# Gate and up products of an expert, interleaved block by block of the contraction

## The reference

```
xe = hf[idx]
hid = jax.nn.silu(jnp.einsum('ecd,edf->ecf', xe, w_gate)) * jnp.einsum('ecd,edf->ecf', xe, w_up)
ye = jnp.einsum('ecf,efd->ecd', hid, w_down) * gates[..., None].astype(h.dtype)
```

## Time and profile before

| | |
|---|---|
| time, median of 3 runs | 1726.99 us (1726.78 to 1728.21) |
| profiled execution, first to last instruction (span) | 1722.5 us |
| what lies around the span, by the runs' median | 4.5 us |
| PE busy, weight loads busy | 1557.6 us, 1324.2 us |
| DVE, ACT, POOL busy | 1111.9, 807.8, 158.4 us |
| mean share of the DMA engines while the experts run | 0.75 to 0.79 |

### The profile page before, as it was taken

One profiled execution on the slowest core, in us unless ns is written; L12 is line 12 of the kernel. 1 busy time (PEld: TensorE's weight loads), 2 busy tenths in 40 slices (PEclk: granted clock), 3 DMA queues, 4 the chain that ended last, 5 costly groups with the idle time before them and its releaser, 6 DMA issues.

```text
span 1722.5 us, 22530 instructions
## 1 busy us (share of the span) xinstructions
PE 1557.6 (90%) x8435; PEld 1324.2 (77%) x8435; DVE 1111.9 (65%) x1529; ACT 807.8 (47%) x1046; POOL 158.4 (9%) x168
## 2 busy tenths in 40 slices
PE   7699999789979878299999999999999999999990
PEld 1588888366748766088899899989988998899880
DVE  2554443647668957747777676777677776767754
ACT  3522332422342232256566665666565655666543
POOL 2011100000000000001011011101110111011100
PEclk9799999989989988689999999999999999999995
DMA  9144341435233135157878777877877787878728
GB/s 348 52 131 127 111 124 61 159 115 191 98 87 84 43 132 192 52 189 229 266 227 256 214 256 237 255 226 249 250 241 239 234 253 228 266 221 249 234 88 311
DMA packets 233220, 324.03 MB, mean 188 GB/s; under 512 B 9892, under 2 KB 193264, under 8 KB 233176
## 3 DMA queue, kind: packets, MB, share of 16 engines
q1 hardware_dynamic: 221784, 297.32, 51.9%
q0 software_dynamic: 9280, 25.47, 7.1%
q10 hardware_dynamic: 2112, 0.66, 0.2%
HBM read 291.90 MB, written 31.51 MB: 188 GB/s over the span
## 4 chain that ended last, share of the span: by engine, by line
PE 78%; DVE 12%; DMA 3%; SPq 2%; ACT 2%; issue 1%; POOL 0%; DVEq 0%; POOLq 0%; ACTq 0%
PE ps L1183 23%; PE ps L926 21%; PE ps L1181 10%; PE ps L1196 4%; PE ps L1200 3%; PE ps L1204 3%; PE ps L1205 3%; PE ps L1197 3%; PE ps L1171 2%; PE ps L1172 2%; DVE idxu L1563 1%; PE ps L1086 1%; DVE aff L1564 1%; PE ps L1186 1%; DVE vals L1561 1%
## 5 line engine op out<-in xcount | busy, mean ns | idle before, releaser
L1183 PE MATMUL ps<-xT,whi 128*128 128x384 f32 x2048 | 577.3, 357 | 1.3 <-DVE xT L1645 1.3
L1639 DVE TENSOR_TENSOR wlo<-raw,whi 128x2048 fp32r<-128x2048 f32 x192 | 437.0, 2290 | 191.6 <-ACT whi L854 191.6
L1181 PE MATMUL ps<-xT,wlo 128*128 128x192 f32 x1792 | 455.7, 254 | 0.0
L1183 PEld LDWEIGHTS ps<-xT,whi 128*128 128x128 f32 x2048 | 368.6, 189 | 2.0 <-issue 1.4
L854 ACT ACTIVATE whi<-raw 128x2048 fp32r<-128x2048 f32 x192 | 361.8, 1901 | 0.0
L1181 PEld LDWEIGHTS ps<-xT,wlo 128*128 128x128 f32 x1792 | 342.9, 191 | 0.0
L926 PE MATMUL ps<-hT,wring 128*128 128x512 f32 x1224 | 284.8, 392 | 8.0 <-DVE hT L1318 5.9
L926 PEld LDWEIGHTS ps<-hT,wring 128*128 128x128 f32 x1224 | 229.5, 189 | 56.7 <-issue 7.0
L926 PE MATMUL ps<-wo,Yhl 128*128 128x512 f32 x576 | 142.1, 410 | 15.4 <-DVE x L1493 10.4
L926 PEld LDWEIGHTS ps<-wo,Yhl 128*128 128x128 f32 x576 | 114.3, 199 | 42.5 <-issue 18.1
L871 ACT ACTIVATE gu_l<-ps 128x384 f32<-128x384 f32 x128 | 62.9, 491 | 160.3 <-PE ps L1183 160.3
(11 more groups left out here) (176 smaller groups left out, 1738.1 us busy)
## 6 DMA issues: line engine op xcount, KB each, us to landing
raw<-in_w_gate SPq DMA_DIRECT2D x64, 1024.0 KB, 5.0
raw<-in_w_up SPq DMA_DIRECT2D x64, 1024.0 KB, 5.8
raw<-in_w_down SPq DMA_DIRECT2D x64, 1024.0 KB, 5.7
wraw<-in_w_in SPq DMA_DIRECT2D x34, 512.0 KB, 4.7
wraw<-in_w_ada SPq DMA_DIRECT2D x32, 512.0 KB, 4.8
ada_w<-in_w_ada SPq DMA_DIRECT2D x8, 1024.0 KB, 15.3
acc_d<-x SPq DMA_DIRECT2D x12, 512.0 KB, 2.7
h_d<-h SPq DMA_DIRECT2D x12, 512.0 KB, 3.9
```

The source lines that it names most:

```text
L1181: pe.matmul(out[:, 0:CAP], wlo[:, slot, w], xT[:, k, 0:CAP], start=False, stop=False, skip_group_check=True)
L1183: mm = pe.matmul(out[:, 0:2 * CAP], whi[:, slot, w], xT[:, k, :], start=k == 0, stop=k == KB - 1, skip_group_check=True)
L1639: dve.tensor_tensor(wlo[:, j % SPL, :], raw[:, j % RAW, :], whi[:, j % SPL, :].bitcast(F32), ALU.subtract).then_inc(w_split, 1)
```

## The change

`gate_and_up` takes the place of `product`. It runs over the eight blocks k once for both products, and for each k issues high gate, high up, low gate, low up. The wait for the gate chunk at even f goes; the wait for the up chunk (which implies the other) now stands ahead of both products. Matmuls, loads, shapes and banks are the same in number and kind; only PE's order and that one wait change.

```
-            def product(out, slot, f):
+            def gate_and_up(b, slots, f):
 
                 for k in range(KB):
                     w = slice(CW * k + P * (f % 2), CW * k + P * (f % 2) + P)
-                    if k:
-                        pe.matmul(out[:, 0:CAP], wlo[:, slot, w], xT[:, k, 0:CAP], start=False, stop=False,
+                    for i, slot in enumerate(slots):
+                        pe.matmul(ps[:, b + i, 0:2 * CAP], whi[:, slot, w], xT[:, k, :], start=k == 0, stop=False,
                                   skip_group_check=True)
-                    mm = pe.matmul(out[:, 0:2 * CAP], whi[:, slot, w], xT[:, k, :], start=k == 0, stop=k == KB - 1,
-                                   skip_group_check=True)
-                    if not k:
-                        pe.matmul(out[:, 0:CAP], wlo[:, slot, w], xT[:, k, 0:CAP], start=False, stop=False,
-                                  skip_group_check=True)
+                    for i, slot in enumerate(slots):
+                        mm = pe.matmul(ps[:, b + i, 0:CAP], wlo[:, slot, w], xT[:, k, 0:CAP], start=False,
+                                       stop=k == KB - 1, skip_group_check=True)
                 return mm
...
                     if f % 2 == 0:
-                        pe.wait_ge(w_split, e * N_CH + (2 * c + 1))
-                    product(ps[:, b, :], 2 * c % SPL, f)
-                    if f % 2 == 0:
                         pe.wait_ge(w_split, e * N_CH + (2 * c + 2))
-                    product(ps[:, b + 1, :], (2 * c + 1) % SPL, f).then_inc(gu_filled, 1)
+                    gate_and_up(b, (2 * c % SPL, (2 * c + 1) % SPL), f).then_inc(gu_filled, 1)
```

## The result

The changed kernel takes 1735.84 us, the kernel before 1726.99 us (medians of 17 runs each); the ratio is 1.0047, with a 95% interval of 1.0037 to 1.0058. The forecast was 1723.7 us, 0.19% faster. The profiled execution took 1737.0 us, with a span of 1735.2 us.

A forecast was written before the change was run, and what follows sets the result against it. The prediction took PE's own stream to bound the kernel. Order -1.7, banks 0, wait 0 and clock -1.6 us summed to -3.3 us, 1727.0 to 1723.7 us, with a range of 1718.3 to 1728.6 us.

The forecast's parts named there:

- What bounds the kernel: Expert work, 741 to 1676 us: only PE's own stream counts; a nanosecond saved between two matmuls is saved from the end.
- The order of the matmuls, -1.7 us: Gate and up: eight seams a step f instead of two products, 13.3 ns less, over 128 steps -1.7 us.
- the seam: Where a product begins in the kernel before: high, high, low, low, taken as 0.5667 us, 2.2 ns under two low-high pairs.
- The lower bound of 0.563 us for a seam: Median over 240 seams between two products; would make the order of the matmuls worth -5.5 us.
- The banks, 0: Output bank changes with every matmul of gate and up, some 3,840 more changes; claimed to cost 0.
- Rival 2: Slower: each change of output bank costs, 11.5 us at 3 ns a change, giving 1736.8 us; chance 0.08.
- a group over 0.569 us: Sign for rival 2 in the changed timeline: two high and two low matmuls taking longer than 0.569 us.
- The wait, 0: PE waits for the up chunk 2.27 us earlier; with 3.5 us of room at the tightest place, cost 0.
- TensorE's clock, -1.6 us: Half-clock stretches behind the transposes, 1.6 us each: one fewer than two, between -3.2 and +1.6 us.
- Rival 4: More half-rate stretches: three more than now, giving 1730.1 us; chance 0.06.
- Rival 1: Order neutral, each load and matmul costs its own: 1727.0 us, or 1725.4 with one half-rate stretch fewer; chance 0.24.
- The sum: -1.7 - 1.6 = -3.3 us from the 1727.0 us median, which stands 4.5 us above the profiled span: 1723.7 us.

The follow-up runs named there:

- the timed pair with halves: Changed kernel and kernel before, each with the next expert's 16 transposes in two halves, behind the first and second calls of down; 1729.44 and 1724.41 us.
- the rotated kernel: Changed kernel with its ring of four turned by one: high gate, low gate, low up, high up; 1723.29 us, 0.9989 of the kernel before.
- the one with two matmuls exchanged: Changed kernel, but each expert's first group (f = 0, k = 0) goes high gate, low gate, high up, low up; 1723.74 us, 0.9988 of the kernel before.
- the kernel with one bank: Changed kernel with the up product added into gate's bank, output of no use; run once, 1736.50 us, an undisturbed expert 58.62 us.

## Why the prediction was wrong, step by step

- **What bounds the kernel.** Right: PE alone; every nanosecond in its stream reached the end, and nothing else did.
- **The order of the matmuls, -1.7 us.** Wrong: +5.6 us by the experts' lengths (16 x 0.35), +5.0 us in the timed pair with halves. The failing step is the sentence that the seam is "just the neighbourhood that the change makes everywhere". The number, 0.567 us a group, was right for that neighbourhood: the rotated kernel and the one with two matmuls exchanged have it, and their 58.17 and 58.18 us are the 58.16 us of the text. But the seam was read in a stream that was in its fast gait, and the change also moved what an expert begins with: high, high behind down's 512 columns, in place of high, low. That tips the stream, and 574 ns a group follow. The forecast took the time of a matmul for a function of its near neighbours ("This holds for each matmul, whatever its neighbours are"); it is not. The lower bound of 0.563 us for a seam was read from the starts of the loads; by the starts of the matmuls the 239 seams at full clock have 567 ns in the median, so the choice of the middle value was right.
- **The banks, 0.** Right; one bank or two makes no difference to the nanosecond. Rival 2, to which the text gave the slower side, named the wrong cause. Its sign, a group over 0.569 us, came true all the same: the sign could not tell a bank's price from any other, and it took the kernel with one bank to do so.
- **The wait, 0.** Right; no new wait of PE appeared.
- **TensorE's clock, -1.6 us.** Wrong in sign, with the wrong length: with expert 0, as the prediction counted, 6 stretches instead of 2 in the profiled executions, +6.4 us, and some +3.3 us in the medians. With experts of 58.17 or 58.18 us there were 1 or 2 (three executions), so the one fewer that was forecast is not shown either. That the number depends on the length of an expert was right, and the upper end (3) was too near: the text let the number move by one upward, as it knew no rows with other lengths. Rival 4, three more stretches, with a chance of 0.06, happened beside the slower order.
- **Rival 1 and the skill's rule.** The Trainium skill, "TensorE: Matmul & The Clock Gate", section "LDWEIGHTS (loading the stationary operand)", gives a load as its columns over 1.2, by estimate 107 ns for 128 columns. The shortest distance of two loads was 107 or 108 ns in all kernels, in both gaits. What differs between the gaits is the distance that a high matmul sets: 174 to 185 ns from load to load in the slow one, 170 to 178 in the fast. So a load's price holds, and the neutral order that I read into it does not.
- **The sum.** The fast gait gives what was forecast, 1723.74 us against 1723.7; but that is luck in good part. The runs of one kernel spread by 6 to 10 us, and the sum took the number of stretches from one execution and its distance to the runs' median, 4.5 us, as fixed, where the time of an execution stands 1.8 us over its own span. The measured 1735.84 us lies outside the range because no case had a stream with a memory, and because the clock's term was taken to be small.

## What to carry to other kernels

In a stream that is bound by PE, the cost of a matmul read at one place holds for the state the stream is in there; before it is multiplied by a thousand, look at what the change puts at the head of the stream, and count on the first matmuls behind another phase. When a long loop slows by a few nanoseconds a matmul, try an exchange of the first two before giving up the order. And try blocks of transposes in halves: in the three kernels that had them so, the clock never fell behind them in the profiled execution, for 0.08 or 0.09 us an expert.

## What the runs showed of the hardware

- In experts 1 to 15 the same alternation of 384 and 192 columns runs at 284.5 or at 290 ns a pair, and high, high, low, low at 567 or at 574 ns, and stays in its gait to the end of an expert's gate and up, 34 us and more. Two 384-column matmuls in a row behind a run of 512-column ones tip it into the slow one, and so do four in a row inside a fast stream; a single one behind the same run does not. Eight transposes or two 512-column matmuls do not bring the fast gait back, 20 of the latter do. What in TensorE holds this state was not found, nor whether fewer than 20 would do. In expert 0, which begins at half clock, one program ran at 567 ns a group in one execution and at 574 in another.
- Stretches at half clock (granted clock 0.5 for 3.4 us, at 1.6 us each) came behind blocks of 16 transposes (3.4 us) and behind none of 8. Their number in fourteen experts ran from 1 to 10 for experts of 58.17 to 59.29 us, and was 4 at 60.99. With a loop 0.35 us longer it went from 2 to 5 in the profiled executions, 4.8 us.
